# A second layer's opening in another order: the last down tile by columns, the norm by columns, the gates later and in four positions

## The chip, the cores and the metric

The kernel runs on one core of a Trainium2 chip. TensorE (PE) multiplies matrices and writes PSUM, VectorE (DVE), ScalarE (ACT) and GpSimd (POOL) work elementwise on SBUF, and SyncE (SP) issues most DMAs. Each engine runs its own program in order and waits on semaphores. The metric is the device time of one execution in microseconds (us), as the median of several runs.

## The reference

Two blocks of two layers each work on 512 patches x 1024 features. The first block's layers also carry 256 context tokens; only the first block is touched here. Cut to what matters:

```python
for l in range(2):
    px = (rmsnorm(x,  norm1_g[l]) * (1 + sc1)  + sh1)  @ w_in[l] + b_in[l]    # patches, 512
    pc = (rmsnorm(xc, norm1_g[l]) * (1 + scc1) + shc1) @ w_in[l] + b_in[l]    # context, 256
    qx, kx, vx, gtx = mlstm_inputs(px)            # gt: 16 gate columns of w_in
    qc, kc, vc, gtc = mlstm_inputs(pc)
    h_c, st_f, st_b = mlstm_bidir(qc, kc, vc, gtc, zs, zs, not last)
    h_x, _, _ = mlstm_bidir(qx, kx, vx, gtx, st_f, st_b, True)
    x = x + g1 * (mix_groups(px, h_x, ...) @ w_out[l])
    x = x + g2 * swiglu(rmsnorm(x, norm2_g[l]) * (1 + sc2) + sh2, w_gu[l], w_down[l])
    if not last: xc = ...                          # the same for the context
```

In the second layer the context is needed only for the keys, the values and the gates.

## The kernel before

Activations lie feature by token: X is [128, 8, 768], eight tiles of 128 features, columns 0 to 511 the patches and 512 to 767 the context. A product is made in three matmuls in a rounded fp32 format: each operand is split into an upper and a lower part, and upper x upper, upper x lower and lower x upper are summed in PSUM. A tile of 768 columns is done in two ranges, 512 and 256. Weights come in tiles of 1024 x 128 by DMA into a ring of four buffers (SP, `load`), and GpSimd splits each in two halves of four k (`split_weights`: a one-element operation L436 that takes the wait, a rounding L441, a subtraction L443, twice). The upper parts have two buffers, so the split of tile n+2 waits until TensorE is done with tile n. The order on each engine is written out by hand.

The first layer ends with eight down tiles (L462 to L465 by `gemm_tile`, k = 6). Of each, ScalarE takes the gated sum out of PSUM (L2019), VectorE adds it to X (L2472), ScalarE squares it (L2025) and VectorE adds the squares up in SS (L2476). The last one is taken by VectorE alone (`add_last_residual`, L2483, patches and then context, and a word of one element, L2486, as signal), squared by ScalarE (L2014). The norm's sum over features is a product with a matrix of ones: SS (L1496) and the last tile's squares (L1499), each for both ranges; then three fillers on TensorE (`keep_running`, L484). ScalarE makes the root (L1952, L1953) for both ranges. VectorE has a dozen small steps of the new layer ahead of its norm (L2510 to L2519). Then for each of eight k: VectorE scales X into a ring Z of four slots (L2383), ScalarE makes the upper part XH with the shift (L1972), VectorE the lower part XL (L2390), each for patches and context.

The layer's in-projection has 24 tiles. Tiles 0 and 1 are done together, k by k behind the norm (`first_pair`, L1646 to L1648). Then come the 16 gate columns (`gates`, L1570 to L1572, 48 matmuls with a stationary of 16 columns; their weights are split by ScalarE and VectorE, L2048 and L2528), evacuated by ScalarE as rows (L2111) and transposed six times (L1578) behind the first half of tile 2. VectorE and ScalarE turn the gates into log forget values; TensorE sums them (`forget_sums`, L1586), transposes them to rows (`gate_rows`, L1599), VectorE scans the rows (L2595 to L2620), and TensorE spreads the result (`columns`, L1605). Between these stand tiles 3 to 8 in halves; the place of each step among the halves is written out in `in_projection`. In the second layer most tiles have the patches' columns only; tiles 6 to 13, keys and values, have both. Between gates, VectorE runs the taps of a convolution (L2464).

Fp32 matmuls are plain, without a split, in the small steps: the sums of ones, the transposes and picks, and the modulation sums (`chunks_summed`, L1519), which put four stationaries of 32 columns side by side in the array by a tile position.

Of the kernel before, what the change touches and what calls it, by code (L numbers as in the profile page):

```python
# [20 lines left out]
P = 128  # L21
# [181 lines left out]
def build_program(nc, xT, cT, cb_d, pc_d, fin_d, srow_d, consts_d, sguw_d, wg_d, wmod_d, win_d, wout_d, wgu_d, wdn_d,  # L203
# [16 lines left out]
    with stack:  # L220
# [40 lines left out]
        wgh = place("wgh", [P, KT, 16], FP32R)  # L261
        wgl = place("wgl", [P, KT, 16], FP32R)
        gt = place("gt", [P, NJ, 2, 2, HEADS])
        lf = place("lf", [P, 3, NJ, 8])
        pick = place("pick", [P, 8], FP32R)
        gcol = place("gcol", [P, NJ, 8])
# [21 lines left out]
        cz2 = place("cz2", [P, KT, 32], addr=addr_of["wgh"])  # L288
# [20 lines left out]
        grow = place("grow", [16, T], addr=addr_of["Z"] + 3 * T * 4)  # L309
# [48 lines left out]
        s_sq = sem("squares_made")  # L358
        s_res = sem("last_residual_first_range_made")
# [7 lines left out]
        s_xl = sem("operand_split")  # L367
        s_dch = sem("dve_chain")
# [11 lines left out]
        s_wgh = sem("gate_weights_upper_made")  # L380
        s_wgl = sem("gate_weights_split")
        s_gate = sem("gates_done")
        s_grow = sem("gate_rows_done")
        s_growe = sem("gate_rows_evacuated")
# [1075 lines left out]
        def _(pool):  # L1460
# [5 lines left out]
            pool.tensor_scalar(identr[:], ident[:], 1.0, 0.0, ALU.mult, ALU.add).then_inc(s_one, 1)  # L1466
            pool.tensor_tensor(pick[:], ident[:, 0:8], ident[:, 32:40], ALU.add)
# [23 lines left out]
        def _(pe):  # L1491
            def norm(q, w):
# [81 lines left out]

            def gates_transposed(l):
                pe.wait_ge(s_growe, l + 1)
                for j in range(NJ):
                    last = pe.transpose(PS[:, 7, 16 * j:16 * j + 16], grow[:, j * P:(j + 1) * P], ident[0:16, 0:16])  # L1578
                last.then_inc(s_gate, 1)
# [97 lines left out]
            def first_pair(l):  # L1677

                n = l * LAYER_TILES
                pe.wait_ge(s_split, 2 * n + 4)  # L1680
                if n:
                    pe.wait_ge(s_evac, n)
                for i in range(KT):
                    pe.wait_ge(s_xl, 2 * KT * l + i + 1)
                    for e in range(2):
# [4 lines left out]
                        if i == KT - 1:  # L1690
                            last.then_inc(s_tile, 1)

            def in_projection(l):
                n0 = l * LAYER_TILES
                first_pair(l)
                gates(l)
                first_half(l, 2)
                gates_transposed(l)
                second_half(l, 2)
                first_half(l, 3)  # L1700
                if l == 0:
                    forget_sums(l)
                second_half(l, 3)
                if l == 0:
                    gate_rows(l)
                first_half(l, 4)
                if l:
                    forget_sums(l)
                second_half(l, 4)
                if l:  # L1710
                    gate_rows(l)
                first_half(l, 5)
                second_half(l, 5)
# [3 lines left out]
                columns(l)  # L1717
                k_transposed(l, 0)
# [5 lines left out]
                k_transposed(l, 1)  # L1724
                second_half(l, 8)
# [171 lines left out]
            for l in range(DEPTH):  # L1897
# [10 lines left out]
                else:  # L1908
                    norm(2 * l, T)
# [7 lines left out]
                for p, (h0, hn) in enumerate(PARTS):  # L1917
# [13 lines left out]
                    def hidden_ready(k):  # L1931
                        pe.wait_ge(s_used, used(s + 2 * k + 1))
                    with pe.Fori(0, 2) as i:
# [7 lines left out]
        def _(act):  # L1941
# [16 lines left out]
            def norm(q, l, w):  # L1958
# [4 lines left out]
                for n, (a, b) in enumerate(ranges(w) if q else [(0, T)]):  # L1963
                    act.wait_ge(s_squ, roots_before(q) + n + 1)
                    rstd(rs[:, a:b], banks(6, 8)[:, a:b], 1.0 / D).then_inc(s_rstd, 1)
                if q == 0:
                    chunks_copied(0, 3, 0)
                act.wait_ge(s_mod, (1, 2, 4, 4)[q])
                for k in range(KT):
                    act.wait_ge(s_xn, KT * q + k + 1)  # L1970
                    for n, (a, b) in enumerate(ranges(w)):
# [5 lines left out]
                act.wait_ge(s_xl, KT * (q + 1))  # L1977

# [24 lines left out]
            def residual_tiles(s0, l, gate, dyn, w, u, q=None):  # L2003

                s = s0 + u
                if u == KT - 1:
                    roots()
                    act.wait_ge(s_acc, sums_before(q) + KT - 2)
                    for n, (a, b) in enumerate(ranges(w)):
# [33 lines left out]
            for l in range(DEPTH):  # L2043
# [3 lines left out]
                act.wait_ge(s_par, 48 * (l + 1))  # L2047
                act.activation(wgh[:], wg[:], ACT.Copy).then_inc(s_wgh, 1)  # L2048
# [58 lines left out]

                in_tile(0, Z[:, 0], ACT.Tanh, 0.5)
                in_tile(1, Z[:, 1])
                act.wait_ge(s_grow, l + 1)  # L2110
                act.activation(grow[:], banks(4, 6)[0:16, 0:T], ACT.Copy).then_inc(s_growe, 1)  # L2111
# [14 lines left out]
                k_tile(0)  # L2126
                gelu_tanh(0)
# [3 lines left out]
                k_tile(1)  # L2131
# [212 lines left out]
        def _(dve):  # L2344
# [25 lines left out]
            def norm(q, l, w):  # L2370
# [5 lines left out]

                def scaled(k):
                    if k >= 4:
                        dve.wait_ge(s_xl, KT * q + k - 3)
                    for n, (a, b) in enumerate(ranges(w)):  # L2380
# [6 lines left out]
                def lower(k):  # L2387
                    dve.wait_ge(s_xh, KT * q + k + 1)
                    for n, (a, b) in enumerate(ranges(w)):
# [17 lines left out]
                lower(KT - 1)  # L2407

# [69 lines left out]
            def add_last_residual(s, l, gate, w, q):  # L2478

                u = KT - 1  # L2480
                dve.wait_ge(s_tile, s + 1)
                for n, (a, b) in enumerate(ranges(w)):
# [487 lines left out]
```

## Time and profile before

| what | value |
|---|---|
| median of 3 runs | 2597.04 us (2594.62 to 2598.04) |
| profiled execution | 2595.66 us, span 2593.8 us |
| TensorE busy | 2522.6 us (97%) |
| VectorE, ScalarE, GpSimd busy | 1389.6, 776.7, 1552.3 us |
| chain that ended last | TensorE 88%, VectorE 4%, issue 3%, others below |
| granted TensorE clock, mean | 0.997 of full speed |

Times in the rows are microseconds from the span's start. A line of a timeline gives start, duration, engine, source line, operation, output and inputs, and in brackets how long the engine idled before and what ended that. A matmul's duration has a tail in which the next one already runs, so the rate is read from starts. A plain fp32 matmul is recorded as two matmuls.

### The profile page before, as it was taken

The numbers are of one execution on the slowest core, as the hardware profiler recorded it, in microseconds if no ns is written. First come the engines' busy times: TensorE is split into PE (matmuls) and PEld (weight loads), VectorE is DVE, ScalarE is ACT, GpSimd is POOL, SyncE is SP. The second block draws the span as 40 slices with busy tenths as digits, with TensorE's granted clock in tenths as the row PEclk, the third lists the DMA queues.
The fourth block names the chain that finished last, engine by engine and source line by source line (L and its number), as shares of the span: only waits on it lengthen the run. The fifth ranks groups of instructions, "written<-read, shape, count | busy, mean of one in ns | idle before, by whom it ended". The sixth has DMA issues, their size and how long they took to land.

```text
span 2593.8 us, 39629 instructions
## 1 busy us (share of the span) xinstructions
PE 2522.6 (97%) x14594; PEld 2084.7 (80%) x14594; DVE 1389.6 (54%) x2062; ACT 776.7 (30%) x1618; POOL 1552.3 (60%) x1625
## 2 busy tenths in 40 slices
PE   5999999999999999999999999999999999999999
PEld 4888988888888886878788887778888888777876
DVE  4865556842853758726433333344444545557754
ACT  3214353111111223245321212222222222443544
POOL 2533345765766665543777777776666676546563
PEclk9999999999999999999999999999999999999999
DMA  6341142332332312121232322433333333323231
GB/s 243 118 172 41 42 171 90 130 123 64 130 130 82 134 60 69 57 59 41 89 97 89 97 92 85 132 106 99 90 105 96 92 103 93 98 72 98 82 106 65
DMA packets 79264, 255.57 MB, mean 99 GB/s; under 512 B 9872, under 2 KB 13712, under 8 KB 78864
## 3 DMA queue, kind: packets, MB, share of 16 engines
q1 hardware_dynamic: 63136, 213.21, 25.4%
q10 hardware_dynamic: 15984, 40.40, 4.9%
q8 instruction: 94, 1.54, 0.2%
q14 instruction: 50, 0.41, 0.0%
HBM read 236.28 MB, written 2.10 MB: 92 GB/s over the span
## 4 chain that ended last, share of the span: by engine, by line
PE 88%; DVE 4%; issue 3%; POOL 2%; ACT 2%; DMA 1%; SPq 1%; ACTq 0%; POOLq 0%; DVEq 0%
PE PS L462 21%; PE PS L465 21%; PE PS L463 21%; PE PS L1646 4%; PE PS L1648 4%; PE PS L1647 4%; PE PS L724 1%; POOL w_lo L443 1%; PE PS L713 1%; PE PS L707 1%; DMA raw<-in_wout 1%; POOL w_hi L441 1%; DVE XL L2390 1%; DMA modt<-in_wmod 1%; PE PS L737 1%
## 5 line engine op out<-in xcount | busy, mean ns | idle before, releaser
L443 POOL TENSOR_TENSOR w_lo<-raw,w_hi 128x512 fp32r<-128x512 f32 (+1 forms) x606 | 883.5, 1458 | 50.6
L462 PE MATMUL PS<-XH,w_hi 128*128 128x512 f32 (+1 forms) x2080 | 781.5, 376 | 17.0 <-DVE XL L2390 3.3
L463 PE MATMUL PS<-XL,w_hi 128*128 128x512 f32 (+1 forms) x2080 | 754.1, 371 | 0.0
L465 PE MATMUL PS<-XH,w_lo 128*128 128x512 f32 (+1 forms) x2080 | 706.1, 372 | 0.0
L436 POOL TENSOR_TENSOR word<-ones 128x1 f32<-128x1 f32 x303 | 98.3, 324 | 869.0 <-PE PS L465 536.2
L462 PEld LDWEIGHTS PS<-XH,w_hi 128*128 128x128 f32 x2080 | 391.3, 188 | 118.6 <-issue 9.3
L441 POOL TENSOR_SCALAR w_hi<-raw 128x512 fp32r<-128x512 f32 (+1 forms) x606 | 482.7, 796 | 0.0
L463 PEld LDWEIGHTS PS<-XL,w_hi 128*128 128x128 f32 x2080 | 391.5, 188 | 69.6
L465 PEld LDWEIGHTS PS<-XH,w_lo 128*128 128x128 f32 x2080 | 361.8, 188 | 55.2
L1646 PE MATMUL PS<-XH,w_hi 128*128 128x512 f32 (+1 forms) x640 | 231.3, 361 | 7.5 <-DVE XL L2390 7.4
L1648 PE MATMUL PS<-XH,w_lo 128*128 128x512 f32 (+1 forms) x640 | 225.5, 352 | 0.0
L1647 PE MATMUL PS<-XL,w_hi 128*128 128x512 f32 (+1 forms) x640 | 225.4, 352 | 0.0
L2472 DVE TENSOR_TENSOR X<-X,Z 128x768 f32 (+3 forms) x60 | 86.3, 1438 | 228.1 <-ACT Z L2019 215.8
L462 PE MATMUL PS<-HH,w_hi 128*128 128x512 f32 (+1 forms) x528 | 187.9, 356 | 3.6 <-DVE HL L2839 3.6
L463 PE MATMUL PS<-HL,w_hi 128*128 128x512 f32 (+1 forms) x528 | 179.0, 354 | 0.0
L2436 DVE CUSTOM_DVE_ANT_0 cprod<-modv,cb 128x1024 f32<-128x1024 f32 x96 | 165.7, 1726 | 17.3 <-DMA modv<-in_wmod 14.4
L465 PE MATMUL PS<-HH,w_lo 128*128 128x512 f32 (+1 forms) x528 | 159.0, 355 | 0.0
L2834 DVE SCALAR_TENSOR_TENSOR Z<-TH,Z 128x768 f32<-128x768 f32 (+1 forms) x44 | 48.7, 1107 | 203.2 <-ACT Z L2000 201.9
L456 POOL TENSOR_TENSOR w_lo<-raw,w_hi 128x512 fp32r<-128x512 f32 x56 | 83.0, 1501 | 106.3 <-ACT w_hi L1046 84.7
L946 ACT ACTIVATE Z<-PS 128x512 f32<-128x512 f32 x99 | 58.8, 595 | 292.4 <-PE PS L465 274.5
L1646 PEld LDWEIGHTS PS<-XH,w_hi 128*128 128x128 f32 x640 | 121.8, 190 | 26.9 <-issue 7.7
L1648 PEld LDWEIGHTS PS<-XH,w_lo 128*128 128x128 f32 x640 | 121.7, 190 | 17.4
(342 smaller groups left out, 3514.2 us busy)
## 6 DMA issues: line engine op xcount, KB each, us to landing
raw<-in_wgu SPq DMA_DIRECT2D x88, 512.0 KB, 3.5
raw<-in_wa SPq DMA_DIRECT2D x80, 512.0 KB, 3.5
modt<-in_wmod SPq DMA_DIRECT2D x48, 512.0 KB, 9.8
raw<-in_win SPq DMA_DIRECT2D x48, 512.0 KB, 3.6
modv<-in_wmod ACTq DMA_DIRECT2D x48, 512.0 KB, 4.8
raw<-in_wdn SPq DMA_DIRECT2D x32, 512.0 KB, 3.5
QS<-Z ACTq DMA_DIRECT2D x96, 128.0 KB, 2.8
raw<-in_wout SPq DMA_DIRECT2D x16, 512.0 KB, 3.6
```

The source lines that it names most:

```text
L436: pool.tensor_tensor(word[:, 0:1], ones[:, 0:1], ones[:, 0:1], ALU.mult)
L441: pool.tensor_scalar(hi, src, 1.0, 0.0, ALU.mult, ALU.add).then_inc(s_hi, 1)
L443: pool.tensor_tensor(lo, src, hi.bitcast(FP32), ALU.subtract).then_inc(s_split, 1)
L456: pool.tensor_tensor(w_lo[s % RING][:, ks, :], src, w_hi[s % 2][:, ks, :].bitcast(FP32), ALU.subtract).then_inc(s_split, 1)
L462: pe.matmul(acc(s)[:, a:b], hi, rh[:, i, a:b], start=i == 0, stop=False)
L463: pe.matmul(acc(s)[:, a:b], hi, rl[:, i, a:b], start=False, stop=False)
L465: last = pe.matmul(acc(s)[:, a:b], lo, rh[:, i, a:b], start=False, stop=i == k - 1)
L1646: pe.matmul(out, hi, XH[:, i, a:b], start=first, stop=False)
L1647: pe.matmul(out, hi, XL[:, i, a:b], start=False, stop=False)
L1648: return pe.matmul(out, lo, XH[:, i, a:b], start=False, stop=i == KT - 1)
L2436: last = dve.tensor_tensor_reduce(out=cprod[:], in0=modv[slots + u][:], in1=cb[:, n, :], scale=0.5, scalar=0.0, op0=ALU.mult, op1=ALU.add, ...
L2472: dve.tensor_tensor(x, x, Z[:, s % 4, 0:w], ALU.add).then_inc(s_used, 1)
```

## The change

In both layers:

- `gates` takes the gate weights unsplit in fp32: four k side by side in four positions of the array, two halves of four k, upper and lower part of the input, two ranges, so 32 matmuls with 32 stationary columns. A stationary of 32 columns holds the 16 of its k and 16 of a neighbour, which are not used. The result is four partial sums on 128 partitions. `grow` grows from 16 to 128 partitions, and the transposes become matmuls with a constant `gsum` that picks and adds the four groups of rows. GpSimd makes `gsum` at the start. The split of the gate weights on ScalarE and VectorE is dropped.
- `first_pair` waits for the first half of tile 1's split, and for its second half at k = 4.

From the first layer's last down tile into the second layer:

- The first layer's last eight down tiles are written out on TensorE. The last of them (`last_down_tile`) makes all patches' columns, signals, makes half of the context's, sums the squares of the patches (SS and the last tile's) and the context's SS, and makes the rest of the context's. The fillers are two.
- VectorE adds the patches' residual, does the layer's small steps, then adds the context's. Its norm makes the patches for all k, then the context for all k.
- ScalarE makes the patches' root, the context's square, four upper parts, the context's root and the other four. The context's upper parts are made three before the evacuation of tiles 0 and 1 and five behind it.
- TensorE sums the context's last squares behind the first pair's k = 1.
- In the second layer the gates move behind tile 2, their transposes behind the first half of tile 3, the forget sums behind the first half of tile 5, the rows behind tile 5, the columns and the first key transpose behind the first half of tile 8. ScalarE evacuates the second key tile ahead of two tanh steps.

The first layer keeps its order. The diff without declarations and the renaming of loops:

```diff
@@ gpsimd
+            pool.tensor_tensor(gsum[:], ident[:, 0:16], ident[:, 32:48], ALU.add).then_inc(s_gsum, 1)
+            for i, c in enumerate((64, 112)):
+                pool.wait_ge(s_gsum, i + 1)
+                pool.tensor_tensor(gsum[:], gsum[:], ident[:, c:c + 16], ALU.add).then_inc(s_gsum, 1)
@@ tensor
+            def down_columns(n, hn, r, k0, k1):
+                a, b = ranges(T)[r]
+                for i in range(k0, k1):
+                    hi, lo = w_hi[n % 2][:, i, :], w_lo[n % RING][:, i, :]
+                    pe.matmul(acc(n)[:, a:b], hi, HH[:, i, a:b], start=i == 0, stop=False)
+                    pe.matmul(acc(n)[:, a:b], hi, HL[:, i, a:b], start=False, stop=False)
+                    last = pe.matmul(acc(n)[:, a:b], lo, HH[:, i, a:b], start=False, stop=i == hn - 1)
+                return last
+            def summed(src, r, first):
+                a, b = ranges(T)[r]
+                return pe.matmul(banks(6, 8)[:, a:b], ones[:], src[:, a:b], start=first, stop=not first)
+            def last_down_tile(n, hn):
+                pe.wait_ge(s_split, 2 * n + 1)
+                pe.wait_ge(s_evac, n - 1)
+                down_columns(n, hn, 0, 0, hn // 2)
+                pe.wait_ge(s_split, 2 * n + 2)
+                down_columns(n, hn, 0, hn // 2, hn).then_inc(s_tilx, 1)
+                down_columns(n, hn, 1, 0, hn // 2)
+                pe.wait_ge(s_acc, sums_before(3))
+                summed(SS[1], 0, True)
+                pe.wait_ge(s_sql, roots_before(2))
+                summed(SQ[1][1], 0, False).then_inc(s_squ, 1)
+                summed(SS[1], 1, True)
+                down_columns(n, hn, 1, hn // 2, hn).then_inc(s_tile, 1)
             def gates(l):
-                pe.wait_ge(s_wgl, l + 1)
-                for k in range(KT):
-                    for a, b in ranges(T):
-                        out = banks(4, 6)[0:16, a:b]
-                        pe.matmul(out, wgh[:, k, :], XH[:, k, a:b], start=k == 0, stop=False)
-                        pe.matmul(out, wgh[:, k, :], XL[:, k, a:b], start=False, stop=False)
-                        last = pe.matmul(out, wgl[:, k, :], XH[:, k, a:b], start=False, stop=k == KT - 1)
+                columns = wg[:].rearrange("p k c -> p (k c)")
+                for a, b in ranges(T):
+                    for half in range(2):
+                        for x in (XH, XL):
+                            for g in range(4):
+                                k = 4 * half + g
+                                at = 16 * (k - (g == 3))
+                                last = pe.matmul(banks(4, 6)[32 * g:32 * g + 32, a:b], columns[:, at:at + 32], x[:, k, a:b].bitcast(FP32),
+                                                 start=half == 0 and x is XH, stop=half == 1 and x is XL, tile_position=(0, 32 * g))
             def gates_transposed(l):
-                    last = pe.transpose(PS[:, 7, 16 * j:16 * j + 16], grow[:, j * P:(j + 1) * P], ident[0:16, 0:16])
+                    last = pe.matmul(PS[:, 7, 16 * j:16 * j + 16], grow[:, j * P:(j + 1) * P], gsum[:], start=True, stop=True)
             def first_pair(l):
+                    if l and i == 1:
+                        pe.wait_ge(s_sql, roots_before(2) + 1)
+                        summed(SQ[1][1], 1, False).then_inc(s_squ, 1)
@@ scalar, norm
-                for n, (a, b) in enumerate(ranges(w) if q else [(0, T)]):
+                for n, (a, b) in enumerate((ranges(w)[0:1] if q == 2 else ranges(w)) if q else [(0, T)]):
+                    root(n, a, b)
+                if q == 2:
+                    act.wait_ge(s_evac, l * LAYER_TILES)
+                    act.activation(SQ[1][1][:, SEQ:T], X[:, KT - 1, SEQ:T], ACT.Square).then_inc(s_sql, 1)
...
+                    if q == 2 and k == 3:
+                        root(1, SEQ, T)
@@ vector, norm
+                def context_scaled(k):
+                    if k >= 4:
+                        dve.wait_ge(s_cxl, k - 3)
+                    dve.scalar_tensor_tensor(out=Z[:, k % 4, SEQ:T], in0=X[:, k, SEQ:T], scalar=nsc[:, 0, k, 1:2], in1=rs[:, SEQ:T],
+                                             op0=ALU.mult, op1=ALU.mult).then_inc(s_cxn, 1)
...
+                for k in range(KT):
+                    context_scaled(k)
+                    if k >= 3:
+                        context_lower(k - 3)
@@ vector, second layer
+                    add_last_residual(n0 - 1, 0, 40, T, 2, 1)
                 norm(2 * l, l, T)
-                dve.wait_ge(s_wgh, l + 1)
-                dve.tensor_tensor(wgl[:], wg[:], wgh[:].bitcast(FP32), ALU.subtract).then_inc(s_wgl, 1)
```

## Rows read from the trace of the kernel before

**Rows 1.** Who TensorE waited for from 975 to 1120: us in total, times, longest
```profile
PE PS L1646 <- DVE XL L2390: 4.2, 4, 2.8
```

**Rows 2.** Timeline of TensorE, 980 to 1004: start, us, engine, line, operation [idle before]
```profile
981.46 1.56 PE L1499 MATMUL PS<-SQ,ones 128*128 128x512 f32 x4 [0.27 <-ACT SQ L2014]
982.86 2.74 PE L484 MATMUL PS<-ones 128*128 128x512 f32 x6
988.42 0.47 PE L1646 MATMUL PS<-XH,w_hi 128*128 128x512 f32 x1 [2.83 <-DVE XL L2390]
...
1003.70 0.39 PE L1648 MATMUL PS<-XH,w_lo 128*128 128x512 f32 x1
```

**Rows 3.** Timeline of TensorE, after the gates
```profile
1012.25 0.39 PE L1646 MATMUL PS<-XH,w_hi 128*128 128x512 f32 x1
...
1015.13 0.54 PE L1578 MATMUL PS<-ident,grow 16*128 16x16 f32 x6
```

**Rows 4.** Timeline of VectorE, around the second layer's norm
```profile
977.68 1.76 DVE L2476 TENSOR_TENSOR SS<-SS,SQ 128x768 f32<-128x768 f32 x1 [0.92 <-ACT SQ L2025]
979.93 1.14 DVE L2483 SCALAR_TENSOR_TENSOR X<-PS,mod,X 128x512 f32<-128x512 f32 x2 [0.49 <-PE PS L465]
980.99 1.19 DVE L2486 TENSOR_TENSOR word<-ones 128x1 f32<-128x1 f32 x1
...
987.13 1.15 DVE L2390 SCALAR_TENSOR_TENSOR XL<-Z,mod,XH 128x512 fp32r<-128x512 f32 x2 [0.19 <-ACT XH L1972]
...
989.25 1.14 DVE L2390 SCALAR_TENSOR_TENSOR XL<-Z,mod,XH 128x512 fp32r<-128x512 f32 x2
```

**Rows 5.** Timeline of TensorE, modulation sums at the kernel's start
```profile
30.78 1.95 PE L1519 MATMUL PS<-modt,cz 128*32 128x128 f32 x64 [2.08 <-DMA modt<-in_wmod]
32.66 0.61 PE L1528 MATMUL PS<-ident,chk 128*128 128x8 f32 x4
```

**Rows 6.** Timeline of ScalarE, the root's first step
```profile
982.63 0.69 ACT L1952 ACTIVATE MT<-PS,eps_c 128x512 f32<-128x512 f32 x1 [0.91 <-PE PS L1499]
```

**Rows 7.** Timeline of GpSimd, splits of in-tiles
```profile
980.04 0.19 POOL L436 TENSOR_TENSOR word<-ones 128x1 f32<-128x1 f32 x1 [1.42 <-PE PS L465]
...
980.90 1.27 POOL L443 TENSOR_TENSOR w_lo<-raw,w_hi 128x512 fp32r<-128x512 f32 x1
...
1003.54 0.19 POOL L436 TENSOR_TENSOR word<-ones 128x1 f32<-128x1 f32 x1 [19.35 <-PE PS L1648]
...
1018.81 0.19 POOL L436 TENSOR_TENSOR word<-ones 128x1 f32<-128x1 f32 x1 [5.70 <-PE PS L1648]
...
1020.09 1.58 POOL L443 TENSOR_TENSOR w_lo<-raw,w_hi 128x512 fp32r<-128x512 f32 x1
```

**Rows 8.** Timelines of GpSimd and VectorE, two places where both work
```profile
1648.46 1.27 POOL L443 TENSOR_TENSOR w_lo<-raw,w_hi 128x512 fp32r<-128x512 f32 x1
...
1648.90 2.04 DVE L1329 SCALAR_TENSOR_TENSOR X<-X,fin_g,TH 128x512 f32<-128x512 f32 x2 [3.17 <-ACT TH L1953]
...
112.03 1.87 POOL L443 TENSOR_TENSOR w_lo<-raw,w_hi 128x512 fp32r<-128x512 f32 x1
...
112.67 2.04 DVE L2547 TENSOR_TENSOR GT<-Z 128x768 f32<-128x768 f32 x1
```

**Rows 9.** Busy time by stretch; the number behind POOL is the granted clock
```profile
989.30:993.00 3.70, 3.70 (x10) 2.46 (x9) 3.70 (x8) 2.25 (x4) 0.00 (x0) 0.54 0.00 0
...
1650.00:1656.00 6.00, 4.24 (x19) 3.46 (x19) 5.97 (x10) 3.16 (x5) 0.00 (x0) 1.00 0.00 0
```

**Rows 10.** Timeline of TensorE, a shorter gap elsewhere
```profile
1651.81 0.48 PE L462 MATMUL PS<-XH,w_hi 128*128 128x512 f32 x1 [1.76 <-DVE XL L1191]
```

**Rows 11.** Timelines of VectorE and TensorE, the selector row of the columns
```profile
1032.35 0.68 DVE L2595 COPY row<-PS 8x512 f32<-8x512 f32 x1 [2.01 <-PE PS L1599]
...
1049.61 1.22 DVE L2620 TENSOR_TENSOR VD<-vrow,ident 8x96 f32<-8x96 f32 x1
...
1051.79 0.46 PE L1605 MATMUL PS<-VD,ones 8*128 8x96 f32 x2
```

More of the change, by code:

```diff
@@ L265, in build_program @@
         pick = place("pick", [P, 8], FP32R)
+        gsum = place("gsum", [P, 16])
         gcol = place("gcol", [P, NJ, 8])
@@ L1695, in in_projection @@
                 first_pair(l)
-                gates(l)
+                if l == 0:
+                    gates(l)
                 first_half(l, 2)
-                gates_transposed(l)
+                if l == 0:
+                    gates_transposed(l)
                 second_half(l, 2)
+                if l:
+                    pe.wait_ge(s_cxl, KT)
+                    gates(l)
                 first_half(l, 3)
@@ L1702, in in_projection @@
                     forget_sums(l)
+                else:
+                    gates_transposed(l)
                 second_half(l, 3)
@@ L1716, in in_projection @@
                 first_half(l, 7)
-                columns(l)
-                k_transposed(l, 0)
+                if l == 0:
+                    columns(l)
+                    k_transposed(l, 0)
                 second_half(l, 7)
@@ L1723, in in_projection @@
                 first_half(l, 8)
-                k_transposed(l, 1)
-                second_half(l, 8)
+                if l:
+                    columns(l)
+                    k_transposed(l, 0)
+                    second_half(l, 8)
+                    k_transposed(l, 1)
+                else:
+                    k_transposed(l, 1)
+                    second_half(l, 8)
                 first_half(l, 9)
@@ L1908, in _ @@
                 else:
-                    norm(2 * l, T)
+                    keep_running(pe, 2)
                 if l == 0:
@@ L1932, in hidden_ready @@
                         pe.wait_ge(s_used, used(s + 2 * k + 1))
+                    if l == 0 and p == len(PARTS) - 1:
+                        for u in range(KT - 1):
+                            gemm_tile(pe, s + 2 * hn + u, HH, HL, T, 0, hn, hidden_ready if u == 0 else None)
+                        last_down_tile(s + 2 * hn + KT - 1, hn)
+                        continue
                     with pe.Fori(0, 2) as i:
@@ L1970, in norm @@
                     act.wait_ge(s_xn, KT * q + k + 1)
-                    for n, (a, b) in enumerate(ranges(w)):
+                    for n, (a, b) in enumerate(ranges(w)[0:1] if q == 2 else ranges(w)):
                         last = act.activation(XH[:, k, a:b], Z[:, k % 4, a:b], ACT.Identity, bias=mods[l][:, 24 * (q % 2) + k, n:n + 1])
@@ L2008, in residual_tiles @@
                     act.wait_ge(s_acc, sums_before(q) + KT - 2)
-                    for n, (a, b) in enumerate(ranges(w)):
+                    for n, (a, b) in enumerate(ranges(w)[0:1] if q == 2 else ranges(w)):
                         if n < len(ranges(w)) - 1:
@@ L2375, in norm @@
                     dve.wait_ge(s_rstd, 1)
+                parts = ranges(w)[0:1] if q == 2 else ranges(w)
                 def scaled(k):
@@ L2379, in scaled @@
                         dve.wait_ge(s_xl, KT * q + k - 3)
-                    for n, (a, b) in enumerate(ranges(w)):
+                    for n, (a, b) in enumerate(parts):
                         if q and k == 0:
@@ L2476, in add_residual, with add_last_residual @@
                     dve.tensor_tensor(SS[1][:, 0:w], SS[1][:, 0:w], SQ[1][u % 2][:, 0:w], ALU.add).then_inc(s_acc, 1)
-            def add_last_residual(s, l, gate, w, q):
+            def add_last_residual(s, l, gate, w, q, part=None):
                 u = KT - 1
-                dve.wait_ge(s_tile, s + 1)
+                dve.wait_ge(*((s_tilx, 1) if q == 2 and part == 0 else (s_tile, s + 1)))
                 for n, (a, b) in enumerate(ranges(w)):
+                    if part not in (None, n):
+                        continue
                     last = dve.scalar_tensor_tensor(out=X[:, u, a:b], in0=acc(s)[:, a:b], scalar=mods[l][:, gate + u, n:n + 1], in1=X[:, u, a:b],
```

58 lines of the change are left out of this document (42 added, 16 removed).

## The prediction

> **What bounds the kernel now.** I read the page first: TensorE is busy almost throughout, so a gain is either less matmul work or less idle time ahead of matmuls. Then the waits of TensorE around the second layer's opening: nearly all of it has one releaser, the norm's lower half of the operand, 4.2 us in four waits [rows 1], none of them behind the pair. The timelines of the engines show why. After the last down tile TensorE sums squares and runs three fillers until 985.6, idles 2.83 us, starts the first pair at 988.42 and issues its last matmul at 1003.70, so the pair is over at 1003.93 [rows 2]. The gates follow until 1012.25: 24 matmuls of 512 columns and 24 of 256 in 8.32 us, which makes 0.231 us for 512 and 0.116 for 256 [rows 2, 3]. So the pair's own 48 matmuls are 11.1 us of the 15.5 it takes: VectorE paces it, with 2.12 us for each of eight k (two operations of 1.06 for 512+256 columns) [rows 4]. Of the 24.0 us from 979.93, when VectorE takes up the last down tile [rows 4], to 1003.93 about 13 are not the pair's matmuls. Behind it TensorE runs without a wait to 1120, so whatever moves before it moves the end.
>
> **The change, part by part.**
>
> *Gates, both layers.* 48 single matmuls become 32 in four column positions, each in plain fp32, two passes. Three fp32 matmuls of 512 take 2.74 us with their tail [rows 2], 0.91 each with it; I take 0.86 without, 0.43 for 256. Four at a time: 4 groups of 0.86 and 4 of 0.43 are 5.2 us. That four do run together is read from the modulation sums, 32 fp32 matmuls of 128 columns in four positions: alone they would take 32 x 0.215 = 6.9 us, the row says 1.95 [rows 5]. With 0.1 for the start I take 5.3, a gain of 3.0 per layer; the end on the other side is no overlap, 20.6 us, far from that row. Behind them six 16-row transposes (0.54 us [rows 3]) become six fp32 matmuls with a 128x128 stationary, 12 passes: between 0.09 each (the transposes' own rate) and 0.15 (the column picks, four such passes in 0.61 [rows 5]), 1.1 to 1.8 us. I take a loss of 0.8. The row copy stays the same length (768 columns per partition) and lies beside the next tile. Net **2.2 us per layer**, 4.4 in all. In layer one nothing else changes on TensorE; the split of tile 2 is made beside the gates and the gates stay longer than it takes, so the 2.2 goes through. The three selector sums on GpSimd and the two dropped weight-split steps lie in idle time: 0.
>
> *The last down tile by columns.* The patches' columns are done 18 x 0.116 = 2.1 us earlier, at 977.9. But VectorE is still in the sum of squares of the tile before until 977.68 + 1.76 = 979.44 [rows 4]: its residual starts at 979.46 instead of 979.93, so only 0.47 of the 2.1 us arrives. With ScalarE's square the squares' matmul moves from 981.46 to 980.99 and the root from 982.63 to 982.16; two steps of 0.7 make it by 983.5 [rows 2, 6]. TensorE, in its new order, waits 0.8 us for the sum and 0.6 for the square, sums (0.86), sums the context's part (0.43) and ends the context's second half (nine matmuls, 1.04) at 983.3. The tile's signal is then at 983.5, call it D, 3.6 us later than before. Behind D stand GpSimd's split of the second in-tile and the context's residual on VectorE.
>
> *The norm by columns.* VectorE's per-layer small steps move ahead of D and are hidden. After D it does the context's residual (0.4), the signal word and then the first product. Here a collision begins. In the rows VectorE operations with two operands in SBUF and GpSimd's split steps exclude each other for a whole operation: the word of one element lasted 1.19 us and ended with GpSimd's subtraction [rows 4, 7]; two products took 2.04, the first held until a subtraction had ended, so the two themselves are 1.21; and where both engines had a queue they took turns, 1.87 for the subtraction and 2.04 for one product of 768 columns [rows 8]. Before, the split (980.04 on) met only small steps and the norm ran clear of it; now it starts at D + 0.1 and meets the norm's first products. Played through with estimates from these rows, under the lock 0.55 for a VectorE operation of 512 columns, 1.15 for the subtraction and 0.5 for the rounding: word at D+0.9, first product to 1.5, subtraction to 2.6, second product to 3.2, rounding to 3.7, first lower half to 4.2, subtraction to 5.4, third product 5.9, second lower half 6.6. The pair starts at D + 4.35 = 987.9, only 0.5 earlier, and its second k at D + 6.7. From there TensorE is the bound: a k needs 1.39 of it and 2 x 0.66 of VectorE (an estimate, 1.06 less the 256 columns). Seven more k and the context's square sum (0.43) end at 1000.4. The second root's detour on ScalarE (square sum, 0.7 until it starts, 1.0, one upper half, one lower half) just meets k = 4.
> [...]
>
> *The clock.* [...] Bounds 0 and 1.2; the gap is nearer to 2.83, so I take the fall: the pair ends at 1001.5, **2.4 us** earlier than 1003.93.
>
> *The gates' old place.* They covered GpSimd's split of tile 2, which starts 0.4 us before the pair ends (1003.54) and needs 2.13 us for a first half free of VectorE, 2.86 beside it (1018.81 to 1021.67) [rows 7]. Now tile 2 is next, and TensorE waits: 1.9 to 2.6 us. VectorE's context products run just then, so I take 2.45, a **loss**. The context's norm (16 operations of 0.4, shared with ScalarE) is done some 5 us after the pair; the gates come 8 us after it.
>
> *What moves later for VectorE.* Its gate chain starts about 4 us later against TensorE. The forget sums, rows and columns are each moved by about a tile for it: from its first row copy to the selector rows VectorE needs 18.5 us (1032.35 to 1049.61 + 1.22), which ends some 52 us behind the pair's end; TensorE uses them at 56, where before the slack was 1 us (to 1051.79) [rows 11]. Zero, and up to 1 us if the slack is misread. SP's fourth weight load and the layer's parameters wait for the tile's signal and the word, some 3.6 us later than now; they are needed by the split of tile 3 and by the gates, some 20 us on. Zero.
>
> **Sum.** 4.4 + 2.4 - 2.45 = 4.4 us. The profiled execution took 2595.66 us (span 2593.8 and 1.9 around it): 2591.3. It lies 1.4 under the median of 2597.04, so the median comes to **2592.6**.
>
> **Rivals.**
> 1. A clean opening: products and split hardly collide and the clock stays. The pair starts at D + 3.1 = 986.6 and ends 11.6 later at 998.3, 5.6 earlier; the wait for tile 2 is 1.9. 4.4 + 5.6 - 1.9 = 8.1: 2588.9. For it: small steps and the 1.76 us gap. Against it: the lock [rows 8]. Chance 0.20.
> 2. The clock falls twice, at the first gap and at the new wait before tile 2 (2.45 us idle, between the 1.76 and the 2.83): another 1.85 us (half of 3.7), 2594.5. This is also where an opening with no gain at all ends. Chance 0.19.
> 3. Slower: the four positions overlap only two by two for 512 columns (the only rows have 128). The gates then take 10.3 us, 2.0 more than now, with the transposes 2.8 per layer; 5.6 + 0 for the opening: 2602.7. It decides from less than 2.7 at a time, where 20.6 us over the overlap plus 0.8 passes 8.3. Against it: the 1.95 us. Chance 0.07.
>
> **How the numbers follow.** Forecast 0.54, rivals 0.20, 0.19, 0.07. Inside the forecast the clock alone moves the time between 2591.4 (no fall, 4.4 + 3.55 - 2.45 = 5.5) and 2592.6, and the transposes and the wait by half a us each way: its own range is 2590.8 to 2593.6. The bound of 0.2%, 5.2 us, about what a measurement can tell from no change, is 2591.85. Faster by more: rival 1 and some 0.16 of the forecast, 0.36. Slower by more: rival 3, 0.07. The rest, 0.57, is within. The range takes in rivals 1 and 2 with half a us at the lower end and, for lost slack behind the gates, 2 us at the upper: 2588.2 to 2596.6.
>
> **What would show it.** The gates' 16 groups: some 5.3 us between their first matmul and the next tile's. The picks behind them: under 2 us. VectorE's first residual at 979.4 counted as here, the last signal of the tile 3.6 us later than now. The first two products beside GpSimd's split: longer than 0.75 each, and an idle TensorE of 2 to 3 us before the pair. A wait of TensorE on the split ahead of tile 2. A first product and split that run beside each other at full length would break the collision; TensorE idle at the columns would break the slack.

## The result and the profile after

The changed kernel takes **2600.62 us** (median of 17 runs, 2596.74 to 2605.53) against 2595.43 for the kernel before on the same chip (17 runs, 2592.50 to 2598.12): a ratio of 1.0020, 95% interval 1.0013 to 1.0026, 5.2 us slower. Forecast were 2592.6 and a range up to 2596.6.

What the opening itself did is read from two views of the changed kernel. First, whom TensorE waited for (us in total, times, longest): the first row is layer one, the rest the second layer's opening, where before nearly all the waiting had one releaser [rows 1].

```profile
PE PS L1624 <- DVE lf L2685: 1.6, 1, 1.6
...
PE PS L1684 <- DVE XL L2472: 3.2, 2, 2.7
PE PS L1684 <- POOL w_lo L445: 1.9, 1, 1.9
PE PS L1608 <- DVE XL L2502: 1.7, 1, 1.7
PE PS L1523 <- DVE SS L2578: 0.6, 1, 0.6
```

Second, TensorE's timeline of the changed kernel (start, us, line, operation, idle before):

```profile
61.54 1.06 PE L1608 MATMUL PS<-XH,wg 128*32 128x512 f32 x8
62.42 1.04 PE L1608 MATMUL PS<-XL,wg 128*32 128x512 f32 x8
...
66.84 0.50 PE L1684 MATMUL PS<-XH,w_hi 128*128 128x512 f32 x1
...
72.52 1.41 PE L1616 MATMUL PS<-gsum,grow 128*128 128x16 f32 x12
...
84.03 0.62 PE L1624 MATMUL PS<-lf,tri 128*128 128x24 f32 x4 [1.58 <-DVE lf L2685]
...
987.06 1.88 PE L486 MATMUL PS<-ones 128*128 128x512 f32 x4
991.65 0.47 PE L1684 MATMUL PS<-XH,w_hi 128*128 128x512 f32 x1 [2.71 <-DVE XL L2472]
...
1007.44 0.50 PE L1684 MATMUL PS<-XH,w_hi 128*128 128x512 f32 x1 [1.93 <-POOL w_lo L445]
...
1015.04 1.06 PE L1608 MATMUL PS<-XH,wg 128*32 128x512 f32 x8 [1.73 <-DVE XL L2502]
...
1020.34 0.50 PE L1684 MATMUL PS<-XH,w_hi 128*128 128x512 f32 x1
```

The gates take 61.54 to 66.84 and 1015.04 to 1020.34, **5.30 us** in both layers, and the picks behind them 1.41: both as forecast. What isn't as forecast is who is late next: the log forget gates in layer one, the context's lower half in layer two.

Neither explains 5.2 us. For that I subtracted the two profiled executions tile by tile: the time at which TensorE signals each of the 331 weight tiles as done, after minus before. The difference moves in seven places:

| where | after minus before, us |
|---|---|
| start to the first pair's end (TensorE waits 23.8 us for the modulation weights' transfers, before 24.8) | -0.50 |
| layer one's opening (tiles 2 and 3) | +0.85 |
| tiles that read HH and HL, in both layers (six stretches) | +3.43 |
| 842 to 856: clock at 0.50 in the changed kernel only | +1.51 |
| second layer's opening (last down tile to tile 10) | -0.45 |
| 1153 to 1157: clock at 0.50 in the kernel before only | -1.56 |
| 2347: a swap by DMA lands later (VectorE stands 12.1 us for it, before 10.6), TensorE waits 1.46 for VT | +1.52 |

Together 4.8, of the 4.9 between the spans (2598.7 and 2593.8). The two entries of the clock need no step of the change: the same waits stand ahead of both falls in both kernels (2.6 us at 843, 1.9 at 1152), and the clock fell behind the one here and behind the other there. Whether the late swap is the change's is open: this tile takes 10.31 us in the profiles of the changed kernel, e4 and e7, and 8.78 to 9.11 in the other eleven, among them all eight with the old last down tile and norm. **The largest entry lies far from the opening, in loops the change doesn't touch:** HH and HL are the upper and lower part of the hidden activations, which the down tiles read, in three stretches of each layer. Two starts of neighbouring tiles show it, each the first matmul of a tile; first the kernel before, HH at 768 columns, XH at 768, HH at 512, XH at 512:

```profile
565.32 0.39 PE L462 MATMUL PS<-HH,w_hi 128*128 128x512 f32 x1
573.64 0.39 PE L462 MATMUL PS<-HH,w_hi 128*128 128x512 f32 x1
...
673.89 0.40 PE L462 MATMUL PS<-XH,w_hi 128*128 128x512 f32 x1
682.29 0.39 PE L462 MATMUL PS<-XH,w_hi 128*128 128x512 f32 x1
...
1375.85 0.39 PE L462 MATMUL PS<-HH,w_hi 128*128 128x512 f32 x1
1381.34 0.39 PE L462 MATMUL PS<-HH,w_hi 128*128 128x512 f32 x1
...
1431.12 0.39 PE L462 MATMUL PS<-XH,w_hi 128*128 128x512 f32 x1
1436.69 0.40 PE L462 MATMUL PS<-XH,w_hi 128*128 128x512 f32 x1
```

and HH's in the changed kernel:

```profile
565.77 0.40 PE L464 MATMUL PS<-HH,w_hi 128*128 128x512 f32 x1
574.17 0.39 PE L464 MATMUL PS<-HH,w_hi 128*128 128x512 f32 x1
...
1377.62 0.39 PE L464 MATMUL PS<-HH,w_hi 128*128 128x512 f32 x1
1383.18 0.40 PE L464 MATMUL PS<-HH,w_hi 128*128 128x512 f32 x1
```

Before, a tile of HH took 8.32 us and one of XH, with the same matmuls, 8.39 to 8.40; at 512 columns 5.49 and 5.57. In the changed kernel HH's take what XH's take. Not one matmul of these loops differs; but `gsum`, 64 bytes per partition, is placed ahead of `work`, so that HH and HL start 64 bytes further on: counted from the first buffer, HH starts at 64 of 256 bytes before and at 128 after. XH starts at 128 in both.

### The profile page after: what moved, and what is told of

The parts are those of the page before. It is cut to its first block, busy times and chain, and to the rows that moved or that the text cites. A ratio compares the mean times of both kernels' runs of the same rounds, so it can differ in the third digit from the quotient of the medians.

```text
span 2598.7 us, 39693 instructions
## 1 busy us (share of the span) xinstructions
PE 2522.4 (97%) x14636; PEld 2083.8 (80%) x14636; DVE 1395.1 (54%) x2060; ACT 775.9 (30%) x1616; POOL 1549.1 (60%) x1628
## 4 chain that ended last, share of the span: by engine, by line
PE 86%; DVE 5%; issue 3%; POOL 2%; ACT 2%; DMA 1%; SPq 1%; ACTq 0%; POOLq 0%; DVEq 0%
PE PS L464 21%; PE PS L467 21%; PE PS L465 20%; PE PS L1684 4%; PE PS L1685 4%; PE PS L1686 4%; PE PS L726 1%; POOL w_lo L445 1%; PE PS L715 1%; PE PS L709 1%; POOL w_hi L443 1%; DMA raw<-in_wout 1%; DVE AC L2566 1%; DMA modt<-in_wmod 1%; PE PS L739 1%
```

## The experiments

The ratios are against the kernel before, run on the same chip beside them. A "tile time" is the distance of the signals of two neighbouring weight tiles within a loop.

**e1: the 64 bytes alone.**

```diff
+        place("pad", [P, 16])
         work = cursor[0]
```

> The kernel before with one unused tile of 64 bytes placed ahead of the region that holds the hidden operand HH, HL; not one instruction differs. Theory 'address': the changed kernel's selector tile of 64 bytes moved HH and HL, and the tiles that read them got slower for that alone: 8.32 us a tile goes to 8.39 at 768 columns, 5.49 to 5.58 at 512 columns, 6.24 to about 6.29 for a down tile; summed over both layers' up, gate and down tiles that is +2.9 us (+2.5 to +3.9). Rival 'instruction stream': the tiles got slower because instructions ahead of the loops were added and removed; then nothing moves here, 0.0 us, 8.32 us a tile.

Measured: 2599.95 us, ratio 1.0016 (1.0007 to 1.0026), +4.5. HH's tiles in its trace:

```profile
564.83 0.40 PE L463 MATMUL PS<-HH,w_hi 128*128 128x512 f32 x1
573.31 0.40 PE L463 MATMUL PS<-HH,w_hi 128*128 128x512 f32 x1
```

8.48 us. The instructions are those of the kernel before, so the instruction stream is out. More than expected: HH's tiles took 8.48, not 8.39, and so did XH's, which were not moved. At 128 a stretch of tiles runs at one of two times, 8.39 or 8.48; which one differs between the profiles, and within the profile of the kernel before from stretch to stretch.

**e2: the changed kernel with its selector behind HH.**

```diff
-        gsum = place("gsum", [P, 16])
 ...
         Ug = place("Ug", [P, 2, T])
+        gsum = place("gsum", [P, 16])
```

> The changed kernel with its 64-byte selector tile placed behind HH and HL instead of ahead of them, all else kept. Theory 'address': tiles of HH come back to 8.32 us, 2.9 us off the changed kernel, so about +2.3 us against the kernel before instead of +5.2. Rival 'instruction stream': the tiles stay at 8.39 us and the time at +5.2.

Measured: 2597.24 us, 1.0006 (0.9997 to 1.0015), +1.8. HH's tiles are back at 8.320 and 5.493 us, and the last down tiles, unrolled by the change, at 6.240 as in the loop before: unrolling costs nothing. So the place of HH is 3.4 us of the 5.2 by the medians (by the two intervals taken together 0.5 to 6.3), 3.43 by the table above; the opening is the remaining +1.8, with an interval that takes in 0, where -4.4 was forecast.

**e3: XH 64 bytes further on.**

```diff
+        place("padx", [P, 16])
         X = place("X", [P, KT, T])
 ...
+        place("pad", [P, 16])
         tri = place("tri", [P, 2, P])
```

> The kernel before with X, XH and XL placed 64 bytes further on and nothing else moved. Theory 'address' in its strong form: it is the place of the moving operand within 128 bytes that counts, so the tiles that read XH go from 8.39 to 8.32 us at 768 columns and from 5.58 to 5.49 us at 512; some 52 and 156 such tiles in loops make 52 x 0.07 + 156 x 0.085 = 17 us less, up to 20 with the straight-line tiles. Weak form (HH moved against something else, its weights or its split): 0. Instruction stream: 0.

Measured: 2602.58 us, 1.0025 (1.0015 to 1.0035): slower, not 17 us faster. The strong form falls. I had overlooked that both pads move HH and the later operand YH too, by 128: all three now start at 192 of 256 bytes, and all three run at 8.373 and 5.600 us. So 128 bytes is the wrong period; over 256 the three kernels agree: HH and YH at 64 fast, all at 128 or 192 slow. That gives the next test.

**e5: XH at 64 as well.**

```diff
-        word = place("word", [P, 8])
-        eps_c = place("eps_c", [P, 2])
         X = place("X", [P, KT, T])
         XH = place("XH", [P, KT, T], FP32R)
         XL = place("XL", [P, KT, T], FP32R)
+        word = place("word", [P, 8])
+        eps_c = place("eps_c", [P, 2])
```

> The kernel before with two small constants (64 bytes) placed behind X, XH and XL instead of ahead of them, so that XH and XL start 64 bytes earlier; no instruction differs. Theory 'place within 256 bytes': HH and YH2 ran at 8.32 and 5.493 us a tile where they started at 64 (mod 256, from the base), at 8.39 to 8.48 and 5.58 to 5.60 where they started at 128 or 192; XH starts at 128 in every kernel up to now but the one at 192. At 64 its tiles go from 8.390 to 8.32 (some 52 of them) and from 5.577 to 5.493 us (some 156): 17 us off, about 2578. Rival 'HH's own': XH's tiles keep 8.39 and 5.577, 2595.4.

Measured: **2578.32 us**, 0.9935 (0.9921 to 0.9948), 16 us off the kernel before with no instruction changed. XH's tiles, 768 and 512 columns:

```profile
671.95 0.39 PE L462 MATMUL PS<-XH,w_hi 128*128 128x512 f32 x1
680.27 0.39 PE L462 MATMUL PS<-XH,w_hi 128*128 128x512 f32 x1
...
1424.71 0.39 PE L462 MATMUL PS<-XH,w_hi 128*128 128x512 f32 x1
1430.21 0.39 PE L462 MATMUL PS<-XH,w_hi 128*128 128x512 f32 x1
```

8.32 and 5.50. In e5 and the five later kernels with HH and XH at 64 no loop ran at another tile time, so small differences show better there.

**p1 and p2: two more places, one run each** (2575.55 and 2600.95 us). p1 is e5 with 192 unused bytes ahead of `work`; p2 is e5 with 64 ahead of `w_hi`, which puts XH at 128, and with two small constants moved behind HH, which keeps HH at 64.

> e5 with HH and HL placed at 0 of 256 bytes instead of 64 (192 unused bytes ahead of them). It measures the fourth place by itself: 5.493 us a tile at 512 columns and 8.32 at 768 if only 128 and 192 are slow, 5.577 to 5.60 and 8.37 to 8.48 if 64 alone is fast. XH's tiles, at 64, stay at 8.32 and 5.493.

> The upper weights w_hi 64 bytes further on, XH back at 128, HH at 64, YH2 at 128. If what counts is the moving operand's own place, XH's tiles take 8.39 to 8.48 and 5.577 to 5.60 us, HH's 8.32 and 5.493, YH2's 5.58 to 5.60. If it is the place against the weights' (64 apart in e5), XH's and YH2's take 8.32 and 5.493 and HH's the slow times.

| start, of 256 bytes: moving operand, upper weights | 768 columns | 512 columns | seen in |
|---|---|---|---|
| 64, 0 | 8.320 | 5.493 | HH before and e2; HH and XH in e5 to e10 |
| 128, 0 | 8.39 or 8.48 | 5.577 or 5.600 | XH before; HH after, e1 and e4 |
| 192, 0 | 8.373 | 5.600 | HH, XH in e3 |
| 0, 0 | 8.427 | 5.440 | HH in p1 |
| 128, 64 | 8.480 | 5.617, 5.547 | XH in p2 |
| 64, 64 | 8.400 | 5.547 | HH in p2 |

Neither of the two simple forms (the operand's own place alone, its place against the weights' alone) holds: 0 is the fastest place at 512 columns and a slow one at 768, and the weights' place counts too, not as a mere difference (64, 64 doesn't run as 0, 0, nor 128, 64 as 64, 0). That the place decides the pace is shown; by what mechanism stays open.

**e4: layer one's forget sums later.**

```diff
-                if l == 0:
-                    forget_sums(l)
-                else:
+                if l:
                     gates_transposed(l)
                 second_half(l, 3)
                 if l == 0:
-                    gate_rows(l)
+                    forget_sums(l)
                 first_half(l, 4)
+                if l == 0:
+                    gate_rows(l)
                 second_half(l, 4)
```

> The changed kernel with layer 1's forget sums one half tile later (behind the second half of the fourth tile instead of its first half) and the gates' rows one half tile later, so that TensorE doesn't stand before VectorE's convolution. Theory 'new wait': the 1.6 us wait and the fall of the clock behind it (0.5 granted from 85.0 to 88.5 us) go, 3.1 us off the changed kernel: about +2.1 us against the kernel before. Rival 'wait moves': VectorE, which stands for the sums later, delays its next products, and TensorE meets the same wait at the gates' rows: +5.2 as before.

Measured: 2601.63 us, 1.0016 (1.0007 to 1.0025), no better than the changed kernel. In the trace the edit did what was expected, 3.3 us less by the seventh tile, without the wait or the fall. Then XH's and HH's tiles at 128 ran at 8.48 instead of 8.39 and took 3.7 back from the 37th to the 79th tile. On that placement a question of 3 us can't be put by medians, so the rest was put with XH and HH at 64.

**e6: the changed kernel, all operands at 64** (the edits of e2 and e5).

> The changed kernel with its selector tile behind HH and with XH, XL 64 bytes earlier: all moving operands where the tiles are fastest and steadiest, so that what is left against e5 is the opening itself. The profile's account of the opening: layer 1 +0.85, layer 2 -0.45, and one fall of the clock more or less (1.5): e5 + 0.4, at most e5 + 2.5. By the prediction's own sum it would be e5 - 4.4.

Measured: 2580.78 us, 0.9947 (0.9933 to 0.9960): e5 + 2.5. Freed of the placement, the opening gives nothing: a loss by the medians, though the runs of the two overlap, and in the two profiles +0.6 us in layer one and +1.4 in layer two. TensorE's waits in it, in layers two and one:

```profile
PE PS L1608 <- DVE XL L2502: 3.7, 1, 3.7
...
PE PS L1684 <- POOL w_lo L445: 1.7, 1, 1.7
...
PE PS L1624 <- DVE lf L2685: 1.5, 1, 1.5
```

The wait for the context is 3.7 here: in this execution the clock didn't fall in the pair, which ended 1.3 us sooner behind the last down tile, and so TensorE came sooner to the wait.

**e7: those waits moved** (e6, e4's edit, and layer two's gates one half tile later).

```diff
                 second_half(l, 2)
+                first_half(l, 3)
                 if l:
                     pe.wait_ge(s_cxl, KT)
                     gates(l)
-                first_half(l, 3)
-                if l:
-                    gates_transposed(l)
                 second_half(l, 3)
+                if l:
+                    gates_transposed(l)
```

> As e6, with the two waits that the prediction didn't have taken off TensorE's way: layer 1's forget sums and gates' rows one half tile later, layer 2's gates behind the first half of the fourth tile instead of ahead of it. Theory 'two waits': 1.6 us and the fall of the clock behind it (1.5) in layer 1, 1.7 us in layer 2: e6 - 3.3 to - 4.8. Rival 'waits move on': e6 within 1.

Measured: **2574.83 us** (2574.16 to 2575.27), 0.9921 (0.9907 to 0.9934): e6 - 6.0, no run of the two within the other's. The rival is out. In the two profiles layer one gives 3.3 of it, the wait and the fall at 85.7 as expected; layer two gives 2.7 and not 1.7, since the wait for the context, 3.7 in e6, is 1.0 here. The fall that e6's profile has behind that wait, at 1007.3, stands in the pair here, at 981.0. TensorE's waits that are left in the two openings:

```profile
PE PS L1684 <- POOL w_lo L445: 1.7, 1, 1.7
...
PE PS L1608 <- DVE XL L2502: 1.0, 1, 1.0
...
PE PS L1624 <- DVE lf L2685: 0.7, 1, 0.7
```

**e8: the gates alone, in their old place** (e5 with the changed kernel's `gates`, `gates_transposed`, `grow` and `gsum`, and layer one's sums as in e4; last down tile and norm as before).

> e5 with one part of the change alone: the gates in four positions, in their old place behind the first pair, in both layers, with the forget sums and rows of layer 1 one half tile later; the last down tile and the norm as in the kernel before. Theory 'the gates alone gain': 2 x (8.32 + 0.54 - 5.30 - 1.41) = 4.3 us, no new wait: e5 - 4.3. Rival 'split late': with the gates 3 us shorter TensorE stands for the lower half of the third tile's weights in layer 2 as the changed kernel does (1.9 us): e5 - 2.4.

Measured: 2577.20 us, 0.9931 (0.9918 to 0.9945): e5 - 1.1. Neither expectation: no wait for the split appears, but the profile's tile 4 of layer two is 4.7 us late against e5's, and TensorE's wait in its trace is, now in layer two, the one that the changed kernel had in layer one:

```profile
PE PS L1596 <- DVE lf L2587: 2.9, 1, 2.9
```

Behind it the clock fell (busy time by engine of a stretch; the number after POOL's is the granted clock):

```profile
1021.00:1024.40 3.40, 3.40 (x9) 2.65 (x8) 1.65 (x5) 0.00 (x0) 0.00 (x0) 0.50 0.00 0
```

**e9: the same with layer two's sums later** (behind `first_half(l, 5)`, rows behind `second_half(l, 5)`, columns as in the changed kernel).

> e8 with layer 2's forget sums three half tiles later, behind the first half of the sixth tile, and its rows and columns where the changed kernel has them. In e8 TensorE stood 2.9 us for the log forget gates there and the clock fell behind it (0.5 granted from 1021.0 to 1024.4 us). Theory 'gates alone gain once the sums stand back': e8 - 2.9 to - 4.4, which is e5 - 4.3 = 2574.0. Rival 'VectorE's gate chain is the bound wherever the sums stand': the wait comes again at the sums, the rows or the columns, e8 within 1.

Measured: **2572.09 us** (2570.20 to 2573.79), 0.9913 (0.9898 to 0.9928): e8 - 5.1, e5 - 6.2, more than the 4.3 of the matmuls. (e9 and e10 ran on another chip than e5 to e8; by the ratios to the kernel before, which take that out, the two differences are -4.7 and -5.7.) In its profile the two openings give 2.8 and 2.2 us, and a fall of the clock at 1149 in e5's, 1.6 us, isn't there. This is the fastest kernel of the study, 23 us under the kernel before, and it has neither the last down tile nor the norm by columns. Against e7, which has both, it is 2.7 us faster (2.1 by the ratios). The second layer's opening accounts for 0.9 of that (against e5's profile -2.2 us in e9, -1.3 in e7); the profiles differ by another 1.5 at the late swap, which e7 has and e9 hasn't, and of which it is open whether the opening causes it.

**e10: the gates of layer two in two parts** (e7 with the patches' columns of the gates right behind the pair, the context's behind `first_half(l, 3)`, sums and rows one half tile later).

> e7 with layer 2's gates cut in two: the patches' columns (3.5 us) right behind the first pair, where TensorE stood 1.7 us for the third tile's lower half of the weights, the context's (1.8 us) behind the first half of the fourth tile, where it stood 1.0 us for the context's lower half; forget sums one half tile later still. Theory 'cover': both waits go, e7 - 2.7, about 2572. Rival 'nothing but moved': VectorE's chain for the gates ends when it did, and TensorE stands for the forget sums as long as it has gained: e7 within 1.

Measured: 2578.39 us, 0.9938 (0.9924 to 0.9951): e7 + 3.6 (4.4 by the ratios), a miss. Both waits went, and two others came, for a bank that ScalarE empties behind its steps for the log forget gates, which stood 7.61 us for VectorE, and for the columns:

```profile
PE PS L1685 <- ACT Z L2127: 2.5, 1, 2.5
PE PS L1644 <- DVE VD L2724: 2.1, 1, 2.1
...
1017.26 0.70 ACT L2194 ACTIVATE lf<-gt 128x8 f32<-128x8 f32 x6 [7.61 <-DVE gt L2673]
```

The clock fell behind both (0.50 from 1020.6 and from 1054.8).

## Why the prediction was wrong, point by point

**Gates in four positions: right in size.** 5.30 us for the forecast 5.3, the picks 1.41 and 1.40 for 1.35. The overlap is complete: a row of two fp32 matmuls of 512 columns takes 1.88 (above), of three 2.74 [rows 2], 0.86 each, and the groups of four start 0.86 to 0.88 apart: four side by side take what one takes. ScalarE's copy of the gates' rows took 0.81 us with 128 partitions, for 0.80 with 16. Rival 3, whose 2602.7 is near the measured time, is out: its mechanism didn't happen.

**"In layer one nothing else changes on TensorE ... so the 2.2 goes through": the first step that failed.** Tile 2 was 2.14 us earlier, as forecast; tile 3 was 2.99 later against that. VectorE's timeline of the changed kernel, with one step of GpSimd's split of tile 4:

```profile
76.53 0.26 DVE L2673 TENSOR_TENSOR gt<-PS,srow 128x96 f32<-128x96 f32 x1
...
76.91 6.24 DVE L2566 SCALAR_TENSOR_TENSOR AC<-YC,pc,AC 128x480 f32<-128x480 f32 x5
...
78.34 1.58 POOL L445 TENSOR_TENSOR w_lo<-raw,w_hi 128x512 fp32r<-128x512 f32 x1
...
83.18 0.26 DVE L2681 TENSOR_SCALAR lf<-gt 128x24 f32<-128x24 f32 x2
```

and the same of the kernel before:

```profile
77.19 4.18 DVE L2464 SCALAR_TENSOR_TENSOR AC<-YC,pc,AC 128x480 f32<-128x480 f32 x5
...
80.93 1.60 POOL L443 TENSOR_TENSOR w_lo<-raw,w_hi 128x512 fp32r<-128x512 f32 x1
...
83.27 1.34 DVE L2577 TENSOR_SCALAR lf<-gt 128x24 f32<-128x24 f32 x2 [1.89 <-ACT lf L2120]
```

VectorE takes the gates up at a fixed place in its convolution, at 76.53 (76.82 before), and the log forget gates five products later. The gates came 3 us earlier and stood waiting. The split of tile 4 starts when TensorE is done with tile 2, so it came 2.6 us earlier too (77.02 for 79.66), and met those five products: they took 6.24 us instead of 4.18, the same in all eight kernels with the short gates (6.24 to 6.26) as in all six with the old ones (4.18 to 4.19). With 4.18 the log forget gates would have been ready at about 81.9 (an estimate from these rows), before TensorE came to the sums at 82.45; so the fixed place alone makes no wait, and this stretch does. TensorE stood 1.58 us at the forget sums, and the clock fell (busy time of a stretch, as above):

```profile
85.00:88.40 3.40, 3.40 (x18) 3.40 (x17) 1.51 (x4) 0.00 (x0) 0.00 (x0) 0.51 0.00 0
```

Granted 0.51 of full speed for 3.4 us: matmuls of 256 columns start 0.21 us apart in it and 0.12 behind it, so about half of it is lost. Before, VectorE itself stood 1.89 us for ScalarE, which follows the end of tile 2, and TensorE came to the sums just as they could start: there was no slack to spend. I had looked for slack behind the gates only in layer two. e4, e7 and e9, with the sums later, show that it is this wait: in their profiles layer one's opening is 2.5 to 3.0 us shorter than in that of the kernel before. That the stretched products cause it is read from the rows; no run has the split moved away.

**Last down tile and norm by columns: right to 0.2 us.** The changed kernel comes to them 3.73 us late (tile 6 of the last eight), which is taken off here: VectorE's sum of squares ends at 979.43 (forecast 979.44), the tile's signal comes at 983.49 (983.5), the pair starts at 987.92 (987.9), the clock falls in it (0.50 from 993.0 to 996.4 in its own times), the pair ends at 1001.6 (1001.5), both counted to the start of the last matmul and 0.23 on. The collision with GpSimd's split was there, two products in 2.42 and a third in 1.76 us. In the rows of the kernel before, a word of one element took 1.19 us and one product of 768 columns 2.04 beside GpSimd's subtraction [rows 4, 7, 8]; that exclusion of the two engines is what the prediction calls the lock.

```profile
988.07 2.42 DVE L2465 SCALAR_TENSOR_TENSOR Z<-X,nsc,MT 128x512 f32<-128x512 f32 x2
...
991.42 1.76 DVE L2465 SCALAR_TENSOR_TENSOR Z<-X,nsc,MT 128x512 f32<-128x512 f32 x1
...
993.77 0.74 DVE L2465 SCALAR_TENSOR_TENSOR Z<-X,nsc,MT 128x512 f32<-128x512 f32 x1
...
1002.93 1.67 DVE L2497 SCALAR_TENSOR_TENSOR Z<-X,nsc,MT 128x256 f32<-128x256 f32 x4
...
1008.45 1.40 DVE L2497 SCALAR_TENSOR_TENSOR Z<-X,nsc,MT 128x256 f32<-128x256 f32 x1
...
1010.93 4.06 DVE L2502 SCALAR_TENSOR_TENSOR XL<-Z,mod,XH 128x256 fp32r<-128x256 f32 x4
```

**The clock: the fall right, its price not measured.** The 2.4 us of the sum have in them 1.1 for a slow stretch of the clock (1001.5 for the pair's end, 1000.4 without it). That price is my estimate, and no run shows it by itself. The profiles show the stretch: 0.54 over 3.7 us behind 2.83 us of idling and none behind 1.76 in the kernel before [rows 2, 9, 10], 0.50 over 3.4 us in the changed kernel's pair, with 2.71 us of idling ahead of it. The second fall of rival 2, behind the wait for tile 2, didn't come: 1.00 from 1007.0 to 1011.0 behind 1.93 us.

**The gates' old place: right, 1.93 for 2.45,** within its bounds. **The context's norm: mis-sized.** "16 operations of 0.4 ... done some 5 us after the pair; the gates come 8 us after it": four products took 1.67, 0.42 each, as long as GpSimd stood still; then GpSimd split tiles 2, 3 and 4 one behind the other and one product took up to 1.40, beside a subtraction of 1.34, the last four lower halves 4.06. All sixteen took 12.1 us, 0.75 each, and ended 9.5 us after the pair; the gates were due 7.8 after it: the wait of 1.73. It is the exclusion that the forecast had read from the rows [rows 4, 7, 8] and used for the first products, and left out sixteen operations later, and in layer one. Put in as measured (pair -2.3, split +1.9, gates and picks -2.1, context +1.7) the terms of the second layer make -0.8, where -0.45 was measured.

**What moved later for VectorE: right.** In the changed kernel's layer two no wait stands at the sums, rows or columns.

**What had no step at all: where the buffers lie.** The prediction priced the three selector sums on GpSimd at 0 and was right in that; the 64 bytes they write cost 3.4 us, through HH's tiles (e1, e2). The parts make 3.4 here, 3.05 in layer one and 1.7 in layer two, 8.2 of the 9.6 between the sum of -4.4 and the measured +5.2; the other 1.4 I don't assign. The profile has 1.5 in the late swap, of which it is open whether the change causes it, and its two entries of the clock cancel.

## What to carry to other kernels

A faster stage pays only where the engine behind it is ready earlier too: ask of every consumer whether it waits for the data or comes at a fixed place of its own queue, and what else starts earlier with the faster stage and collides with that queue, in each layer where the change applies. Keep the matmuls' operands where they are when a small buffer is added (put it behind them), and before a question of a few us is put, see that the untouched loops of the two traces run at the same tile time. Where an operation collides with another engine, price all of its repetitions under the collision, not the first ones alone.

## What was not expected of the hardware

The pace of the same matmuls in the rounded fp32 format (fp32r in the rows) depends on where their operands start, in steps of 64 bytes within 256 of a partition as far as these runs tell: 8.32 to 8.48 us for a tile of 768 columns, 5.44 to 5.62 for one of 512, 16 us of this kernel between XH at 128 and at 64. At 128 two paces occur, between stretches of one profile and between profiles; at 64 the loops of six kernels ran at one. That the pace at 128 changes between executions of one kernel fits the spread of the runs (2594.15 to 2604.78 in e1, 2577.19 to 2580.98 in e5) but isn't shown, as each kernel has one profile. After the same wait the clock sometimes fell and sometimes didn't: behind 2.6 us at 843 it stayed at 1.00 in the profile of the kernel before and was at 0.50 from 846.2 in that of the changed one. The trace of the kernel before had both cases, no fall behind that 2.60 us and one from 1153.3 behind 1.87; the prediction read two other gaps, 2.83 with a fall and 1.76 without [rows 2, 9, 10], and took the length as the sign.
